# Gated scan: the products of the 32 and 64 levels on column tiles of TensorE

## The reference, cut to what matters

```python
def step(S, xs):
    qc, kc, vc, bc = xs
    diff = bc[:, :, :, None, :] - bc[:, :, None, :, :]
    diff = jnp.where(causal[None, None, :, :, None], diff, -jnp.inf)
    A = jnp.einsum('bhtd,bhsd,bhtsd->bhts', qc, kc, jnp.exp(diff))
    o = (jnp.einsum('bhts,bhsv->bhtv', A, vc)
         + jnp.einsum('bhtd,bhdv->bhtv', qc * jnp.exp(bc), S))
    b_last = bc[:, :, -1:, :]
    S = (jnp.exp(b_last[:, :, 0, :])[..., None] * S
         + jnp.einsum('bhsd,bhsv->bhdv', kc * jnp.exp(b_last - bc), vc))
    return S, o
```

## Time and profile before

| what | value |
|---|---|
| device time, median of 3 runs | 1473.64 us (1472.53 to 1474.77) |
| device time of the profiled execution | 1471.87 us |
| its span, first to last instruction | 1470.0 us |
| TensorE busy | 1438.5 us, 98% of the span |
| VectorE busy | 873.6 us, 59% |
| ScalarE busy | 565.6 us, 38% |
| chain that ended last | TensorE 95%, VectorE 3%, DMA 1%, ScalarE 1% |
| granted TensorE clock, mean | 0.998 |

### The profile page before, as it was taken

How to read it: one execution, slowest core, us unless ns; L and a number is a source line. 1 busy time by engine, 2 the same in 40 slices (tenths; PEclk the granted TensorE clock), 3 DMA queues, 4 the chain that set the end, 5 groups by cost and what they waited for, 6 DMA issues and landing times.

```text
span 1470.0 us, 18495 instructions
## 1 busy us (share of the span) xinstructions
PE 1438.5 (98%) x7204; PEld 1202.7 (82%) x7204; DVE 873.6 (59%) x1720; ACT 565.6 (38%) x1027; POOL 0.2 (0%) x4
## 2 busy tenths in 40 slices
PE   4999999999999999999999999999999999999998
PEld 4788888888888888988888888888888888888886
DVE  7887776543333336656557445325878777787645
ACT  5423355423233324533333234333444444444341
POOL 0000000000000000000000000000000000000000
PEclk9999999999999999999999999999999999999999
DMA  8646541353332334124224233232222221221221
GB/s 334 222 168 238 178 138 63 119 199 98 101 93 94 101 100 129 58 86 126 75 86 128 80 109 101 86 100 72 72 62 69 72 72 60 71 72 60 85 72 58
DMA packets 43863, 158.31 MB, mean 108 GB/s; under 512 B 4864, under 2 KB 5248, under 8 KB 43776
## 3 DMA queue, kind: packets, MB, share of 16 engines
q1 hardware_dynamic: 43776, 157.12, 32.5%
HBM read 155.00 MB, written 2.10 MB: 107 GB/s over the span
## 4 chain that ended last, share of the span: by engine, by line
PE 95%; DVE 3%; DMA 1%; ACT 1%; issue 0%; SPq 0%; ACTq 0%; DVEq 0%
PE PS L498 29%; PE PS L500 28%; PE PS L499 28%; PE PS L782 1%; PE PS L830 1%; PE PS L793 1%; PE PS L494 1%; PE PS L834 1%; PE PS L824 1%; PE PS L802 1%; PE PS L810 1%; DVE RAW L947 1%; PE PS L849 1%; DMA X<-in_x 1%; DMA RAW<-in_ada 0%
## 5 line engine op out<-in xcount | busy, mean ns | idle before, releaser
L498 PE MATMUL PS<-HH,WH 128*128 128x512 f32 (+1 forms) x1088 | 430.7, 396 | 0.0
L500 PE MATMUL PS<-HH,WL 128*128 128x512 f32 (+1 forms) x1088 | 418.3, 384 | 0.0
L499 PE MATMUL PS<-HL,WH 128*128 128x512 f32 (+1 forms) x1088 | 417.2, 383 | 0.0
L983 DVE TENSOR_TENSOR WL<-RAW,WH 128x1024 fp32r<-128x1024 f32 x219 | 266.2, 1219 | 70.2 <-ACT WH L1691 69.9
L1691 ACT ACTIVATE WH<-RAW 128x1024 fp32r<-128x1024 f32 x219 | 230.7, 1057 | 172.9 <-PE PS L500 138.5
L500 PEld LDWEIGHTS PS<-HH,WL 128*128 128x128 f32 x1088 | 204.4, 188 | 42.1
L498 PEld LDWEIGHTS PS<-HH,WH 128*128 128x128 f32 x1088 | 204.8, 188 | 37.1
L499 PEld LDWEIGHTS PS<-HL,WH 128*128 128x128 f32 x1088 | 205.0, 188 | 36.0
L498 PE MATMUL PS<-WH,ZH 128*128 128x512 f32 x400 | 155.9, 390 | 0.0
L500 PE MATMUL PS<-WH,ZL 128*128 128x512 f32 x400 | 155.6, 389 | 0.0
L499 PE MATMUL PS<-WL,ZH 128*128 128x512 f32 x400 | 155.6, 389 | 0.0
(11 more groups left out here) (263 smaller groups left out, 1774.5 us busy)
## 6 DMA issues: line engine op xcount, KB each, us to landing
RAW<-in_w_fc SPq DMA_DIRECT2D x64, 512.0 KB, 3.5
RAW<-in_hgrn_in SPq DMA_DIRECT2D x64, 512.0 KB, 3.5
RAW<-in_ada SPq DMA_DIRECT2D x43, 512.0 KB, 4.4
RAW<-in_pool_in SPq DMA_DIRECT2D x40, 512.0 KB, 3.6
RAW<-in_w_in SPq DMA_DIRECT2D x27, 512.0 KB, 4.7
RAW<-in_pool_out SPq DMA_DIRECT2D x16, 512.0 KB, 3.6
RAW<-in_hgrn_out SPq DMA_DIRECT2D x16, 512.0 KB, 3.5
RAW<-in_w_out SPq DMA_DIRECT2D x8, 512.0 KB, 3.5
```

What stands on the lines that cost most here:

```text
L498: e.matmul(out, wh, xh, start=first, stop=False)
L499: e.matmul(out, wh, xl, start=False, stop=False)
L500: return e.matmul(out, wl, xh, start=False, stop=last)
L983: e.tensor_tensor(lo, raw(i), hi.bitcast(F32), ALU.subtract).then_inc(taken.sem, taken(i))
```

## The change

On TensorE the eight products of level 32 no longer all write to partitions 0 to 31 of the bank, side by side over 256 columns. Product i writes to partitions 32 * (i % 4) onwards and columns 32 * (i // 4) onwards, so that the start partition, which is the column tile of the array, goes round 0, 32, 64, 96. The four products of level 64 go by turns to partitions 0 and 64. The numbers of matmuls, their operands and their order stay. ScalarE gathers the results from the new places with four copies of 32 x 64 instead of two of 32 x 128, and two of 64 x 128 instead of one of 64 x 256.

```diff
                 k0, q1 = halves(t.k, 32)[0], halves(t.q, 32)[1]
                 for i in range(8):
-                    m = e.matmul(PS[b][0:32, 32 * i:32 * i + 32], k0[:, i, :], q1[:, i, :], start=True, stop=True)
+                    r, c = 32 * (i % 4), 32 * (i // 4)
+                    m = e.matmul(PS[b][r:r + 32, c:c + 32], k0[:, i, :], q1[:, i, :], start=True, stop=True)
                 m.then_inc(banks.full[b], banks.fill(("level", h, 32), b))
...
                 k0, q1 = halves(t.k, 64)[0], halves(t.q, 64)[1]
                 for i in range(4):
-                    m = e.matmul(PS[b][0:64, 64 * i:64 * i + 64], k0[:, i, :], q1[:, i, :], start=True, stop=True)
+                    r, c = 64 * (i % 2), 64 * (i // 2)
+                    m = e.matmul(PS[b][r:r + 64, c:c + 64], k0[:, i, :], q1[:, i, :], start=True, stop=True)
                 m.then_inc(banks.full[b], banks.fill(("level", h, 64), b))
...
                 b = level_bank(h, 32)
-                pair = PS[b][0:32, 0:256].rearrange("p (i n l) -> p i n l", n=2, l=32)
-                e.activation(t.diag[0:32, :, 32:64], pair[:, :, 0, :], ACT.Copy)
-                e.activation(t.diag[64:96, :, 96:128], pair[:, :, 1, :], ACT.Copy).then_inc(banks.free[b], 1)
+                for i in range(4):
+                    to, r = 64 * (i % 2), 32 * i
+                    m = e.activation(t.diag[to:to + 32, i // 2:4:2, to + 32:to + 64],
+                                     PS[b][r:r + 32, 0:64].rearrange("p (i l) -> p i l", l=32), ACT.Copy)
+                m.then_inc(banks.free[b], 1)
                 yield
                 b = level_bank(h, 64)
                 e.wait_ge(*banks.made(("level", h, 64)))
-                e.activation(t.diag[0:64, :, 64:128], PS[b][0:64, 0:256].rearrange("p (i t) -> p i t", i=4),
-                             ACT.Copy).then_inc(banks.free[b], 1)
+                for i in range(2):
+                    m = e.activation(t.diag[0:64, i:4:2, 64:128],
+                                     PS[b][64 * i:64 * i + 64, 0:128].rearrange("p (i t) -> p i t", i=2), ACT.Copy)
+                m.then_inc(banks.free[b], 1)
```

## The result

The changed kernel takes 1464.89 us (median of 4 runs, 1463.35 to 1465.63) against 1473.97 us for the kernel before beside it (1472.53 to 1474.77). The ratio is 0.9941, 95% interval 0.9929 to 0.9952: 0.6% faster, 9.1 us between the medians, where 1.7 us were forecast and 1467.0 was the lower end of the range. The profiled execution of the changed kernel has a span of 1461.5 us, 8.5 us less than before.

What follows compares the result with a forecast made beforehand. TensorE's own work was taken to bound the kernel; 28 + 78 = 106 ns a head, times 16, made 1.7 us, so 1473.64 - 1.7 = 1471.9 us, with a range of 1467.0 to 1476.5 us.

Steps and rivals of the forecast that it cites:

- What bounds the kernel: In the scan TensorE is busy for all 379 us, so a nanosecond counts only if it is TensorE's own.
- Where the steps come from: Levels 32 and 64: weight load and streaming take equally long, 27 and 54 ns; steps are 3 to 4 ns longer.
- The gaps around narrow blocks: TensorE's array empties for 0.09 us before and after narrow work; 0.2 us a block that the change leaves.
- slower rival: On a change of tile the weight load isn't hidden: 5.0 us slower, 1478.7 us, or 1493 with emptying; chance 0.11.
- rival with one path for weights: Loads go one at a time or tiles don't overlap: 0.6 us saved at most, 1473.0 to 1473.6 us; chance 0.28.
- Part 1: Level 32 on four tiles: 7 of 15 steps change tile, each falling from 31 to 27 ns; 28 ns a head.
- Part 2: Level 64 on two tiles: 3 of 7 steps change tile, each falling from 57 to 31 ns; 78 ns a head.
- Part 3: ScalarE's copies of levels 32 and 64 take 0.5 us a head more, 8 us in all, costing nothing on the path.
- rival of deep overlap: TensorE goes on while a low pass waits in its tile: 2.9 to 6.5 us saved, 1467.1 to 1470.7; chance 0.19.

## Why the prediction was wrong

- **What bounds the kernel** was right: the gain is TensorE's own time, ns for ns.
- **Where the steps come from** was half right. A 32-column pair takes 31 ns and a 64-column pair 57 ns, because load and stream are equally long; but I then took the 31 ns for the rate at which TensorE can issue pairs. It was the pace of one tile. The next tile's product starts after 7 ns, which is 3.3 ns a pair, and no row of before could show it, since there every pair had to wait for the tile.
- **The gaps around narrow blocks** stayed, as said, and a change of tile costs none. The slower rival fell. The 0.2 us a block leave out the next wide load in the open, 0.11 us more (1165.95 - 1165.61 - 0.23). The rival with one path for weights leaned on loads that never overlap by more than their tails; but at level 32 a load of 0.11 us began 31 ns after the one before it, so the rows never showed that.
- **Part 1** failed at "the engine takes them in program order", so that 7 of 15 steps were to change tile. All 15 do, because TensorE runs the first passes of four products ahead of the second ones. The term was 28 ns a head and is 0.36 us. Order and price share the miss: 7 steps from 31 down to 7 ns would have given 168 ns, and the rest is the order.
- **Part 2** failed at the same place, with 3 of 7 steps, and at the 31 ns that each of them was to fall to: 78 ns forecast, 0.23 us in the chain. Three steps from 57 down to 7 ns would have given 150 ns.
- **Part 3** was right: 48 more copies within 4 ns of the forecast durations, and no wait on the path.
- **The range** missed because even the rival of deep overlap put 31 ns, or half of it, under every step, 6.5 us at most. The right bound was the tile's own work divided by the number of tiles, 16 x 31 ns = 0.50 us over four tiles and 8 x 57 ns = 0.46 us over two: 0.37 + 0.23 = 0.60 us a head, 9.6 us. I had the numbers for it and chose the row of the serial pace instead. The estimate from the Trainium skill, "TensorE: Matmul & The Clock Gate", Part 3, Measured speedup vs the span model, 4.3 us for level 32 at 2.38 times, was nearer than my term, and level 32 alone gave 4.9 us; this level's load steps got 0.47 / 0.11, over four times as short: 15 steps of one tile became three rounds of the four tiles and three starts of 7 ns.

## What to carry to other kernels

A plain fp32 product with 32 or 64 columns of weights leaves the other column tiles idle; spread consecutive products over the start partitions 0, 32, 64, 96 (or 0 and 64) and price it as the work of the busiest tile plus a fixed 0.3 us around each narrow block. It can even pay to cut a wide product into narrow ones where only the blocks on the diagonal are wanted: two such cuts saved another 15 us here, and the results landed on the partitions where VectorE's masked copies want them, at the price of one more masked copy a head. Issue the tiles in turn, put narrow blocks side by side, and then look at who must have the next operands ready.

## What the runs showed of the hardware

- TensorE starts matmuls out of program order between column tiles: 0 1 2 3 0 1 2 3 for passes that the program holds as 0 0 1 1 2 2 3 3.
- The first matmul on the next tile starts 6.7 ns after the one before when two load and matmul pairs lie between them in the program, and 13.3 ns when four do: 3.3 ns a pair.
- One tile takes a new pair of 32 columns every 31 ns and of 64 every 57 ns; with 32 to load it is 31.6 ns for 16 columns streamed and 42.5 ns for 48.
- It goes past three waiting passes on each busy tile, nine in all, and three is likely the limit; eight in a row for one tile cost 15.5 us over 32 blocks.
- The gaps before and after narrow work, with the open load of the next wide weights, cost about 0.3 us a block on one, two or four tiles alike.
